# Gate-up weights in two transfers of 4 MB per expert and down in one, with down's rows dealt to eight units

## The reference

```python
logits = ht @ w_router + b_router                 # 32 experts, 4 per token
top_logits, top_idx = lax.top_k(logits, TOP_K)
gates = jax.nn.softmax(top_logits, axis=-1)
...
gu = xb @ w_gate_up[e] + b_gate_up[e]             # (1024, 2048) per expert
gate = jnp.minimum(gu[..., :D_FF], SWIGLU_LIMIT)
up = jnp.clip(gu[..., D_FF:], -SWIGLU_LIMIT, SWIGLU_LIMIT)
act = (up + 1.0) * (gate * jax.nn.sigmoid(gate * SWIGLU_ALPHA))
return act @ w_down[e] + b_down[e]                # (1024, 1024) per expert
```

## Time and profile before

| | |
|---|---|
| median of 3 runs | 1248.43 us (1248.24 to 1248.56) |
| the profiled execution | 1248.27 us |
| its span, from the first instruction to the last | 1246.4 us |
| PE busy | 1172.7 us (94%) |
| read from HBM | 452.74 MB |

### The profile page before, as it was taken

How to read it: one execution, slowest core, us unless ns; L and a number is a source line. 1 busy time by engine, 2 the same in 40 slices (tenths; PEclk the granted TensorE clock), 3 DMA queues, 4 the chain that set the end, 5 groups by cost and what they waited for, 6 DMA issues and landing times.

```text
span 1246.4 us, 15481 instructions
## 1 busy us (share of the span) xinstructions
PE 1172.7 (94%) x6198; PEld 619.5 (50%) x6198; DVE 389.6 (31%) x703; ACT 276.1 (22%) x421; POOL 7.5 (1%) x27
## 2 busy tenths in 40 slices
PE   9999999999999999989989999899999998999996
PEld 8998887898633433333333333333433333333432
DVE  5987677546312111111111112102111111112112
ACT  5655566345211101010000101001101011011102
POOL 1000000000000000000000000000000000000000
PEclk9999999999999999999999999989999999999999
DMA  9454333469899999999999999999999999999996
GB/s 344 151 203 142 129 135 137 161 262 379 314 416 428 429 429 429 427 428 428 427 429 429 429 429 429 429 427 428 429 429 428 429 428 429 427 416 429 428 426 256
DMA packets 56966, 454.28 MB, mean 364 GB/s; under 512 B 6556, under 2 KB 6724, under 8 KB 30948
## 3 DMA queue, kind: packets, MB, share of 16 engines
q1 hardware_dynamic: 56752, 453.74, 88.2%
q10 hardware_dynamic: 180, 0.07, 0.0%
HBM read 452.74 MB, written 1.05 MB: 364 GB/s over the span
## 4 chain that ended last, share of the span: by engine, by line
PE 56%; DMA 41%; DVE 1%; issue 1%; SPq 1%; ACT 0%; DVEq 0%; POOL 0%; POOLq 0%
DMA ring<-in_moe_w_down 41%; PE ps L952 14%; PE ps L980 11%; PE ps L615 3%; PE ps L617 3%; PE ps L616 3%; PE ps L630 2%; PE ps L990 2%; PE ps L631 2%; PE ps L632 2%; PE ps L928 2%; PE ps L602 1%; PE ps L747 1%; PE ps L967 1%; PE ps L726 1%; PE ps L725 1%
## 5 line engine op out<-in xcount | busy, mean ns | idle before, releaser
L980 PE MATMUL ps<-ring,wring 128*64 128x512 f32 x960 | 216.5, 597 | 53.0 <-DMA ring<-in_moe_w_down 53.0
L952 PE MATMUL ps<-ring,wring 128*64 128x512 f32 x1024 | 223.5, 594 | 0.0
L1101 ACT ACTIVATE wring<-ps 128x512 f32<-128x512 f32 (+2 forms) x101 | 52.4, 534 | 496.2 <-PE ps L952 424.1
L980 PEld LDWEIGHTS ps<-ring,wring 128*64 128x64 f32 x960 | 65.1, 137 | 192.6 <-issue 112.2
L1828 DVE COPY wring<-ps 128x512 f32<-128x512 f32 x32 | 22.1, 692 | 402.7 <-PE ps L952 402.7
L952 PEld LDWEIGHTS ps<-ring,wring 128*64 128x64 f32 x1024 | 72.0, 137 | 139.3 <-issue 139.1
L1836 DVE TENSOR_TENSOR wring<-ps,bguT 128x512 f32<-128x512 f32 x64 | 41.2, 686 | 300.8 <-PE ps L967 300.8
L952 PE MATMUL ps<-mid,wring 128*64 128x512 f32 x512 | 115.2, 603 | 1.0 <-DVE wring L1836 1.0
L1101 ACT ACTIVATE ysb<-ps 128x512 f32<-128x512 f32 x36 | 21.4, 595 | 264.6 <-PE ps L980 250.3
L952 PEld LDWEIGHTS ps<-mid,wring 128*64 128x64 f32 x512 | 36.0, 139 | 69.0 <-issue 69.0
L928 PEld LDWEIGHTS ps<-wring 128*128 128x128 f32 x480 | 55.8, 192 | 23.5 <-issue 23.5
(11 more groups left out here) (316 smaller groups left out, 1416.0 us busy)
## 6 DMA issues: line engine op xcount, KB each, us to landing
ring<-in_moe_w_gate_up SPq DMA_DIRECT2D x60, 2048.0 KB, 23.1
ring<-in_moe_w_down SPq DMA_DIRECT2D x59, 2048.0 KB, 25.5
mid<-in_moe_w_gate_up SPq DMA_DIRECT2D x31, 2048.0 KB, 23.5
wring<-in_moe_w_gate_up SPq DMA_DIRECT2D x15, 2048.0 KB, 26.3
hs<-in_moe_w_gate_up SPq DMA_DIRECT2D x15, 2048.0 KB, 27.9
wring<-in_ssd_w_in SPq DMA_DIRECT2D x9, 2048.0 KB, 8.1
ring<-in_moe_w_down SPq DMA_DIRECT2D x10, 1024.0 KB, 33.1
wring<-in_xa_w_kv SPq DMA_DIRECT2D x4, 2048.0 KB, 8.0
```

The costliest lines, as they stand in the source:

```text
L952: last = mm(ps[a][SLOTS * half:SLOTS * (half + 1), :], xs[:, m, c % 2, :], w[:, kk, c0:c0 + 512], start=s + kk == 0, stop=s + kk == GP)
L980: last = mm(ps[D_BANK][SLOTS * half:SLOTS * (half + 1), :], act[:, k, :], w[:, kk, 512 * half:512 * (half + 1)], start=k == 0, stop=k == K ...
L1101: return nc.scalar.activation(out_, in_, func, **kw)
```

## The change

Gate-up's eight slices are grouped by four (GR = 4): row 4p + k of a block of 512 rows lies on partition p, and two neighbouring pieces form a group of 4 MB, 32 KB per partition, that one transfer fills. Down's rows are taken by eight: row 8p + k lies on partition p, again 32 KB per partition, and one transfer of 4 MB fills both of down's pieces. For the odd experts the pieces are renumbered so that two neighbours lie side by side on chip (`odd_ring`). The transfers of 4 MB raise the semaphore of their first piece alone, so the waits for the second pieces are for older counts.

SP's waits follow: a group of gate-up is asked for when both of its pieces have been used, down when both of its pieces have been used. The first experts are loaded in pieces and rows as before, and expert 3, expert 31 and the last two downs too.

As a unit of down's input now has eight neighbours on a partition, gate-up's output columns are dealt by eight: the streamed operand of each `gate_up` matmul takes four floats and leaves four (`dealt`), half 0 the first four, half 1 the second. The order of the gathered slices (k), of the norm's output (in fours) and of the bias transposes (eight of 64 columns in place of four of 128) follows.

```diff
@@ sizes @@
+GR = 4
+GJ = 2 * GP // GR
+GS = GR // 2
@@ gu_slot @@
-            return (part(mid, 0, WP), part(mid, WP, 2 * WP), wslot[2], hs[:, :])[n - GP]
+            return part(odd_ring, WP * (n - GP), WP * (n - GP + 1))
...
-        gu_dram = w_gate_up.rearrange("e (s p k) n -> e s p k n", p=P, k=2)
-        dn_dram = w_down.rearrange("e (s p k) n -> e s p k n", p=P, k=4)
+        def gu_group(odd, j):
+            base = part(odd_ring, 0, GP * WP) if odd else part(ring, 0, GP * WP)
+            return base[:, GS * WP * j:GS * WP * (j + 1)].rearrange("p (k n) -> p k n", k=GR)
+
+        gu_rows = w_gate_up.rearrange("e (j p k) n -> e j p k n", p=P, k=GR)
...
+        dn_rows = w_down.rearrange("e (p k) n -> e p k n", k=KD)
...
+        def load_down_whole(sp, e):
+            whole = part(ring, GP * WP, (GP + DP) * WP).rearrange("p (k n) -> p k n", k=KD)
+            sp.dma_start(whole, dn_dram(e, 0, KD)).then_inc(d_ready[0], 16)
...
+        def load_gate_up_group(sp, e, odd, j):
+            sp.dma_start(gu_group(odd, j), gu_rows[e, j, :, :, :]).then_inc(g_ready[GP * odd + GS * j], 16)
@@ SP @@
-            def reload_gate_up(e, i, c, pieces_=range(GP)):
-
-                for s in pieces_:
-                    sp.wait_ge(gu_used, 2 * GP * i + (GP * (c - 2) + s + 1))
-                    load_gate_up(sp, e, c % 2, s)
+            def reload_gate_up(e, i, c, groups=range(GJ)):
+
+                for j in groups:
+                    sp.wait_ge(gu_used, 2 * GP * i + (GP * (c - 2) + GS * (j + 1)))
+                    load_gate_up_group(sp, e, c % 2, j)
 
             def reload_down(e, i, c):
 
-                for s in range(DP):
-                    sp.wait_ge(dn_used, 2 * DP * i + (DP * (c - 1) + s + 1))
-                    load_down(sp, e, s)
-
-            with sp.Fori(0, PAIRS - 4, 1) as i:
+                sp.wait_ge(dn_used, 2 * DP * i + DP * c)
+                load_down_whole(sp, e)
+
+            reload_pieces(3)
+            reload_down(1, 0, 1)
+            reload_gate_up(4, 0, 4)
+            reload_down(2, 0, 2)
+            with sp.Fori(1, PAIRS - 4, 1) as i:
                 for c in (1, 2):
                     reload_gate_up(2 * i + (c + 2), i, c + 2)
                     reload_down(2 * i + c, i, c)
-            reload_gate_up(NE - 5, 0, NE - 5, (0, 1))
+            reload_gate_up(NE - 5, 0, NE - 5, range(0, GJ // 2))
             reload_down(NE - 7, 0, NE - 7)
-            reload_gate_up(NE - 5, 0, NE - 5, (2, 3))
-            for e in range(NE - 6, NE - 2):
+            reload_gate_up(NE - 5, 0, NE - 5, range(GJ // 2, GJ))
+            for e in range(NE - 6, NE - 3):
                 reload_down(e, 0, e)
                 reload_gate_up(e + 2, 0, e + 2)
+            reload_down(NE - 3, 0, NE - 3)
+            reload_pieces(NE - 1)
@@ TensorE, gate_up @@
-                                c0 = 1024 * a + 512 * half
-                                last = mm(ps[a][SLOTS * half:SLOTS * (half + 1), :], xs[:, m, c % 2, :],
-                                          w[:, kk, c0:c0 + 512], start=s + kk == 0, stop=s + kk == GP)
+                                dealt = w[:, kk, 1024 * a:1024 * (a + 1)].rearrange("p (q h j) -> p h q j", h=2, j=4)
+                                last = mm(ps[a][SLOTS * half:SLOTS * (half + 1), :].rearrange("p (q j) -> p q j", j=4),
+                                          xs[:, m, c % 2, :], dealt[:, half, :, :], start=s + kk == 0, stop=s + kk == GP)
@@ TensorE, gathers; bias transposes; VectorE, norm @@
-                    k = 4 * (m // 2) + 2 * half + m % 2
+                    k = 4 * (m % 2) + 2 * (m // 2) + half
...
-                for n in range(4):
-                    last = tr(ps[5][:, n * P:(n + 1) * P], bg_rows.rearrange("p (q j) -> p j q", j=4)[:, n, :], ident)
+                for n in range(8):
+                    last = tr(ps[5][:, 2 * NE * n:2 * NE * (n + 1)],
+                              bg_rows[0:2 * NE, :].rearrange("p (q j) -> p j q", j=8)[:, n, :], ident[0:2 * NE, 0:2 * NE])
...
-                    v.scalar_tensor_tensor(out=dst[:, t, :].rearrange("q (k p) -> q k p", k=2),
+                    v.scalar_tensor_tensor(out=dst[:, t, :].rearrange("q (k p) -> q k p", k=GR),
```

More of the change, by code:

```diff
@@ L83, in build @@
         sq_at = hs_at + 4 * 2048
+        assert mid_at == wring_at + 12 * WP and hs_at == mid_at + 8 * WP
         def part(base, first, end, r=None, **sizes):
@@ L133, in build @@
         rows_b = part(ring, 20608, 20736)
-        bg_rows = part(ring, 10240, 10752)
+        bg_rows = part(ring, 11264, 12288)
         xn0 = part(ring, 4096, 6144, r="p (t n) -> p t n", t=TC)
@@ L476, in _ @@
                 for half in range(2):
-                    rows = slice(2 * half, 2 * half + 2)
-                    sp.dma_start(dn_last(n)[:, rows, :],
-                                 dn_dram[NE - 2 + n // DP, n % DP, :, rows, :]).then_inc(dl_ready[2 * n + half], 16)
+                    k0 = 4 * (n % DP) + 2 * half
+                    sp.dma_start(dn_last(n)[:, 2 * half:2 * half + 2, :],
+                                 dn_dram(NE - 2 + n // DP, k0, k0 + 2)).then_inc(dl_ready[2 * n + half], 16)
             sp.wait_ge(lst_ok, 1)
@@ L937, in scatter_transpose, with gate_up @@
                 last.then_inc(st_ps, 1)
-            def gate_up(i, c, first=False):
+            def gate_up(i, c, expert, first=False):
                 for s in range(GP):
@@ L1034, in regular @@
                 pe.wait_ge(up_b, 2 * i + c)
-                gate_up(i, c)
+                gate_up(i, c, expert)
                 if gathers:
```

66 lines of the change are left out of this document (40 added, 26 removed).

## The result

The changed kernel takes 1256.74 us (median of 9 runs, 1254.3 to 1263.07) against 1248.43 in the same comparison: a ratio of 1.0069 (1.0058 to 1.0080), 8.3 us slower. The forecast had the sign and 3.5 us, less than half of it; its range of 1245.5 to 1257.0 just holds the time. The profiled execution took 1256.88 us, its span 1255.1 against 1246.4.

The account below looks back on a forecast made before the run. The prediction took the stream of weight transfers as the bound, 29.364 us per expert with TensorE 3.3 us to spare. It summed 1248.27 + 6.7 + 1.6 - 4.8 = 1251.8 us, 0.3% slower, range 1245.5 to 1257.

Parts of the forecast that it names:

- After expert 16: Loads after expert 16's biases and list: next gate-up group issued with 1.3 us notice, a hole of 1.6 us.
- Part 2: Queue fed in larger steps: whole-down waits put TensorE 3.37 us later against the landing; holes of 1.6 and 6.7 us.
- Part 4: Small edits (bias transposes, row load over 64 partitions, norm in fours): nothing, to 0.5 us.
- Early: Load of expert 4's gate-up: 3.7 us of notice, so no hole, at worst 0.4 us.
- the last loads: End of the weight stream: no term of its own; the last orders stay 2 MB and 1 MB as before.
- the change of order: Before expert 26's down, asked for ahead of gate-up: it waits for all of expert 25's; a hole of 6.7 us.
- The notice: DMA queue: a transfer must be issued 2.9 us before its predecessor lands; later issue opens a hole as long.
- Part 1: Weight loads of 4 MB instead of 2 MB: each saves 58 ns in packets, 83 of them 4.8 us.
- Part 3: Gate-up's matmuls reading four floats and leaving four: taken as free; bounds nothing and 1.49 times.
- No hole: Rival, faster: holes do not open at expert 26's down, only the saving is left, 1243.4 us; chance 0.15.
- Packets that save nothing: Rival on the weight stream: larger packets gain nothing as the engines' rate is that of bytes; 1256.6 us; chance 0.14.
- TensorE as the bound: Rival on gate-up's matmuls: the dealt operand slows TensorE past the stream; about 1350 us at 1.49 times; chance 0.05.
- A fixed cost per transfer: Rival on the weight stream: 2.6 us latency per transfer goes for 83 of them, 216 us; about 1033; chance 0.01.

Follow-up runs that it names:

- 16 KB runs: Changed kernel with its 4 MB transfers, each partition's 32 KB read from memory as two runs of 16 KB; 1260.56 us in one run.
- after: The changed kernel itself as profiled, against the kernel before the change; median 1256.74 us, ratio 1.0069.
- norm by twos: Changed kernel with the norm ahead of the experts reading every second float as before, not every fourth; 1255.69 us, ratio 1.0067.
- halves at the change of order: Changed kernel with down in two halves, each with its own wait, for experts 25 to 29 alone; 1254.02 us, ratio 1.0042.
- three idle matmuls: Changed kernel plus three unread matmuls ahead of down's wait for experts 6 to 15 and 18 to 23; 1255.91 us, ratio 1.0062.
- six: Changed kernel plus six idle matmuls on TensorE ahead of each down's wait, up to expert 23; 1262.22 us, ratio 1.0118.
- halves up to expert 24: Changed kernel with down loaded and awaited in 2 MB halves up to expert 24, whole from 25 to 29; 1250.85 us, ratio 1.0024.
- load two places later: Against down in halves: gate-up's biases loaded two places later, their eight transposes on TensorE later too; 1245.95 us, ratio 0.9985.
- halves and norm: Against down in halves: the norm ahead of the experts reads in natural order and writes with a step; 1246.45 us, ratio 0.9988.
- biases in two: Against down in halves: gate-up's biases loaded in two transfers of 2 KB rows instead of one of 4 KB rows; 1247.50 us, ratio 0.9993.
- load one place later: Against down in halves: gate-up's biases loaded one place later, behind the mixer weight's third piece; 1248.69 us, ratio 1.0002.
- down in halves: Changed kernel with down again two 2 MB transfers, each with its own wait, gate-up still in 4 MB groups; 1247.07 us, ratio 0.9994.
- whole down and 2 MB pieces: Changed kernel with gate-up in 2 MB pieces, each asked for when its own piece is used, down still whole; 1257.46 us, ratio 1.0071.

## Why the prediction was right, and where it was wrong

The sum came out at less than half of the loss; the mechanism was right, and sizes were not. The steps that failed are "After expert 16" of Part 2 (1.6 us for 4.2), Part 4 (nothing to 0.5 for 2.3 at the front), "Early" (nothing for 1.2) and the last loads, which had no term (0.7).

**Right in mechanism: what bounds the kernel, the two places, the change of order.** The stream sets the time; the queue runs empty after expert 16 and before expert 26's down, near 829 and 1097 as said; the second hole was 6.3 us with its forerunner, for 6.7. Expert 26's down was asked for at T + 33.1, where the forecast had T + 33.0. The notice that was taken as 2.9 us came out as 12.0 - 9.71 = 2.3 and 12.8 - 9.71 = 3.1 at the two holes.

**Part 1 was mis-sized by a little.** A 4 MB transfer saves 75 ns and not 58, within the bounds given (5.1 to 9.4 ns per packet; it is 9.4). 83 of them are 6.2 us. The run with 16 KB runs shows that it is the packets.

**Part 2, "After expert 16", is the step that failed most.** It had TensorE 3.37 us later against the landing and all else as before: issue at T + 27.9, a hole of 1.6. The issue came at T + 29.5, and the holes were 3.5 and 0.7. The 3.4 us were right. What it had wrong is that all else would take as long as before: TensorE stood at the lower clock for 10.2 us there, from the list into gate-up, where it had been 6.8 before, and gate-up took 16.64 us in place of 15.72. The kernels with 4 MB groups of gate-up, by how down came up to expert 16, how long the clock stood at the lower level around the list, and when the next group was asked for (T is the landing of expert 15's down):

| down | lower level, us | issue |
|---|---|---|
| whole: after; norm by twos | 10.2 | T + 29.5 |
| whole: 16 KB runs | 6.8, and 3.4 in expert 15's down | T + 29.2 |
| whole: halves at the change of order; three idle matmuls; six | 6.8 | T + 28.0; 27.8; 28.2 |
| halves: halves up to expert 24; load two places later | 13.7 | T + 27.6 |
| halves: halves and norm; biases in two; load one place later | 10.2 | T + 25.9 |
| halves: down in halves | 6.8 | T + 24.6 |

The lower stretch in three of the traces, length first and clock third from the end: after, halves at the change of order, the load two places later.

```profile
815.60:825.90 10.30, 7.75 (x28) 3.22 (x29) 2.36 (x12) 0.39 (x1) 0.00 (x0) 0.50 0.98 423
```

```profile
818.20:825.00 6.80, 4.53 (x18) 1.90 (x20) 2.18 (x11) 0.38 (x1) 0.00 (x0) 0.50 1.00 429
```

```profile
808.80:822.50 13.70, 11.19 (x33) 4.35 (x33) 2.32 (x12) 0.38 (x1) 0.00 (x0) 0.50 0.97 417
```

Between whole and halves with the same stretch lie 3.2 to 3.6 us, the forecast's term; between 6.8 and 10.2 us of the lower clock lie 1.3 to 1.7, which is what it lacked. With 6.8 us the first hole was 1.8 (halves at the change of order) and 1.1 (three idle matmuls), near the 1.6 forecast. That down's longer wait made this stretch longer is not shown. Down in halves has 6.8, 10.2 and 13.7 as well, after a clock that was up from 335 us to the list, and in after the wait ahead of expert 15's down was 1.64 us and that down ran at the higher level. What sets the stretch stays open.

In the loop the long wait did bring the clock down, and there it cost nothing, as the stream sets the pace; I had read the steady wait as cover that costs nothing, and it did cost where such a wait stood just ahead of a tight place: 3.0 us in the run with whole down and 2 MB pieces. The 0.7 us behind the hole is not an empty queue: that transfer was issued at 846.17, 6.8 us before the one ahead of it landed. What held it stays open.

**Part 2, "Early: nothing, at worst 0.4"**, was 1.2. The margin of 3.7 us there was counted from before's front; with the front 2.3 us later, and first gathers that took 4.45 us instead of 2.92 (329.15 before, 331.12 after) at the lower clock, part of it was gone: 2.9 us of notice were left at expert 4, and the hole was 0.8. The 0.4 at expert 5 is not a late issue (8.2 us of notice) and stays open. In the run with the biases moved, where down comes in halves, the loads of experts 4 and 5 have no hole (one of 1.3 us stands at expert 3's).

**Part 4, "Nothing, to 0.5 us", is wrong.** The norm's step costs 0.8 us per instruction (what that is worth in the whole time is within the noise of the run by twos); the biases' load makes the mixer's second piece 1.2 us late, and the experts' norm starts 1.2 us late. That it does so because it lies on half as many partitions is argued, not shown. I had counted elements, and not the order in which they are read, nor what else is in the queue beside a load.

**Part 3 was right:** 594 ns with and without the step, for runs of four floats with four left out. The Trainium skill (Advanced Engine Details and Errata, Memory Cachelines) says that accesses that stay in one 16-byte line have full performance, and this trace agrees. The same section asks for two accesses to a line and penalises a new line for each; the norm's instruction, with two floats to a line before and one after, agrees: 1.28 us, and 2.10. I had weighed the rule for TensorE, and not for the norm, where it decides.

**The rivals.** No hole: gone, by 5.7 us. Packets that save nothing: its time was met and its mechanism was not there (29.14 per expert, not 29.36). TensorE as the bound: only where six idle matmuls made it so (28.81 us of work per expert without a wait). A fixed cost per transfer: 16 KB runs in 4 MB transfers kept the old pace, so there is none.

**What stays open:** why the load on 64 partitions makes the neighbouring piece late (row length is excluded); what sets how long the clock stays down around the list; the 0.7 us behind the hole there; and the 0.7 us ahead of the last loads.

## What to carry to other kernels

Joining transfers is two changes: the transfer gets faster by its packets, here 75 ns each, and the buffer comes free, and the consumer starts, later by half its work, here 3.4 us each way. Take the first where the queue stays full (gate-up) and leave the second where it is tight (down): halves for down and 4 MB for gate-up gave 0.9994, and 0.9985 with the biases out of the way. And when a wait moves, ask what its new length does to the engine that waits: two short waits (53.0 us in all) left the clock up in the loop, and one long one (43.6) did not. Where the queue is full that is free; where it is tight, 32 matmuls that take 8.4 us or more instead of 7.0 make the next issue as much later.

## What the runs showed of the hardware that I had not expected

- One wait of some 3 us per expert was followed, in many turns, by a granted clock at the lower level, and 32 matmuls took 8.4 to 10.1 us instead of 7.0; with waits of up to 1.8 us, twice as many and more in sum, the clock stayed at the higher level up to the list.
- Around the list, where TensorE and VectorE wait for each other, the clock stood at the lower level for 6.8, 10.2 or 13.7 us also in traces of kernels whose code from 335 us up to there is the same; from each of these lengths to the next, the next load was asked for 1.3 to 1.7 us later.
- A read of every fourth float takes VectorE 2.10 us per 1024 elements, and a write whose neighbouring floats land 256 apart 2.02, against 1.28 for a read of every second float.
- A 256 KB load on 64 partitions, issued behind a 2 MB piece, made that piece land 1.2 us later than the same bytes on 128 partitions did, whether in one transfer of 4 KB rows or two of 2 KB.
